# Attention of neighbouring heads in the two partition halves, logits in the output banks

## What is computed

```python
# fox branch, for one block of 128 queries
logits = einsum('bthd,bshd->bhts', qb, k) * HEAD_DIM ** -0.5 + fb - cum_k
p = softmax(where(key_pos <= t_pos, logits, NEG))
o = einsum('bhts,bshd->bthd', p, v)
# latent branch: the same with keys and values expanded from a latent of 128,
# a T5 bias, and all but the top 64 keys of each query masked by a score
```

## Time and profile before

| | |
|---|---|
| median of the runs | 1445.54 us |
| the profiled execution | 1447.23 us, its span 1445.1 us |
| PE (matmul) busy | 1403.2 us, 97% of the span |
| DVE, ACT, POOL busy | 939.4, 785.2, 134.6 us |
| DMA | 243 MB, mean 168 GB/s |

### The profile page before, as it was taken

One profiled execution on the slowest core, in us unless ns is written; L12 is line 12 of the kernel. 1 busy time (PEld: TensorE's weight loads), 2 busy tenths in 40 slices (PEclk: granted clock), 3 DMA queues, 4 the chain that ended last, 5 costly groups with the idle time before them and its releaser, 6 DMA issues.

```text
span 1445.1 us, 23849 instructions
## 1 busy us (share of the span) xinstructions
PE 1403.2 (97%) x8845; PEld 1249.3 (86%) x8845; DVE 939.4 (65%) x1451; ACT 785.2 (54%) x1376; POOL 134.6 (9%) x223
## 2 busy tenths in 40 slices
PE   5999989999999999999999999999999999999997
PEld 5888879988999888888888888899989999888886
DVE  4666665867566557666676666658666566666665
ACT  5455555755554556555565555565547445655543
POOL 2010000022320100000000000000224001000001
PEclk9999999999999999999999999999999999999999
DMA  8678664543435555666566567445344454465661
GB/s 219 190 202 210 187 181 146 176 146 129 152 129 176 174 143 155 198 180 198 175 177 201 175 188 214 141 154 168 120 154 136 146 184 145 138 204 176 199 180 71
DMA packets 286064, 243.38 MB, mean 168 GB/s; under 512 B 14280, under 2 KB 263544, under 8 KB 285984
## 3 DMA queue, kind: packets, MB, share of 16 engines
q1 hardware_dynamic: 283856, 236.77, 53.7%
q10 hardware_dynamic: 1600, 4.25, 0.8%
q0 software_dynamic: 528, 1.26, 0.6%
HBM read 241.18 MB, written 1.27 MB: 168 GB/s over the span
## 4 chain that ended last, share of the span: by engine, by line
issue 62%; PE 29%; DVE 3%; POOL 1%; ACT 1%; DMA 1%; POOLq 1%; DVEq 1%; ACTq 0%
PE work L1507 17%; PE work L1582 2%; PE work L1727 2%; PE work L1529 2%; PE work L1716 2%; PE work L1584 1%; PE acc L1544 1%; POOL diag L702 1%; PE work L1707 1%; DVE score L1308 1%; POOLq L701 1%; DMA gains_in<-in_mem_norm 1%; PE work L1651 0%; PE acc L1458 0%; DVE w_lo L504 0%
## 5 line engine op out<-in xcount | busy, mean ns | idle before, releaser
L504 DVE TENSOR_TENSOR w_lo<-raw,w_hi 128x1024 fp32r<-128x1024 f32 x444 | 537.7, 1231 | 104.2 <-ACT w_hi L496 102.3
L1582 PE MATMUL work<-act,w_hi 128*128 128x512 f32 x1408 | 499.4, 398 | 8.3 <-DVE w_lo L504 4.3
L496 ACT ACTIVATE w_hi<-raw 128x1024 fp32r<-128x1024 f32 x444 | 452.5, 1052 | 26.0 <-PE acc L1544 25.6
L1584 PE MATMUL work<-act,w_lo 128*128 128x256 f32 x1408 | 395.8, 281 | 0.0
L1582 PEld LDWEIGHTS work<-act,w_hi 128*128 128x128 f32 x1408 | 265.3, 188 | 72.9 <-issue 9.3
L1507 PE MATMUL work<-act,w_hi 128*128 128x256 f32 x1696 | 317.2, 286 | 4.7 <-DVE o_lo L1366 2.2
L1507 PEld LDWEIGHTS work<-act,w_hi 128*128 128x128 f32 x1696 | 267.5, 192 | 12.4 <-issue 6.3
L1584 PEld LDWEIGHTS work<-act,w_lo 128*128 128x128 f32 x1408 | 267.0, 190 | 1.6
L1507 PE MATMUL work<-act,w_lo 128*128 128x256 f32 x848 | 239.8, 283 | 0.0
L803 ACT ACTIVATE gu_s<-work 128x256 f32<-128x256 f32 x176 | 58.0, 382 | 209.6 <-PE work L1584 209.6
L1507 PEld LDWEIGHTS work<-act,w_lo 128*128 128x128 f32 x848 | 162.5, 192 | 0.1
(11 more groups left out here) (232 smaller groups left out, 1771.6 us busy)
## 6 DMA issues: line engine op xcount, KB each, us to landing
raw<-in_ffn_w_gu SPq DMA_DIRECT2D x176, 512.0 KB, 4.9
raw<-in_w_in SPq DMA_DIRECT2D x52, 1024.0 KB, 5.0
raw<-in_ffn_w_down SPq DMA_DIRECT2D x44, 1024.0 KB, 4.8
raw<-in_w_branch SPq DMA_DIRECT2D x12, 1024.0 KB, 4.9
raw<-in_w_mkv SPq DMA_DIRECT2D x8, 1024.0 KB, 5.1
raw<-in_w_out SPq DMA_DIRECT2D x8, 1024.0 KB, 4.8
raw<-in_w_mq SPq DMA_DIRECT2D x4, 1024.0 KB, 5.0
raw<-in_w_mo SPq DMA_DIRECT2D x4, 1024.0 KB, 4.9
```

Source lines behind the costliest of these rows:

```text
L496: eng.activation(halves(w_hi, slot, kind, part), halves(raw, slot, kind, part), ACT.Copy)\
L504: eng.tensor_tensor(halves(w_lo, slot, kind, part), halves(raw, slot, kind, part), halves(w_hi, slot, kind, part).bitcast(F32), ALU.subtra ...
L1582: pe.matmul(work[:, 2 * c + g, :], w_hi[:, slot, at_w:at_w + P], act[:, :, k, :], start=(k == 0), stop=False, skip_group_check=True)
L1584: mm = pe.matmul(work[:, 2 * c + g, 0:SEQ], w_lo[:, slot, at_w:at_w + P], act_hi[:, k, :], start=False, stop=(k == KT - 1), skip_group_che ...
```

## The change

The two heads of a stream slot become neighbours, 2·pr and 2·pr+1, one in each half of the partitions, in the same tile. The logits go to `acc`, one bank for each head, two banks for even slots and two for odd; the `qk` jobs leave the turn of the `work` banks, and PE waits for the extreme (`lg_ready`) of slot s-2 instead of a bank. The two `pv` products write the two halves of the partitions, the same columns, and their order is chunk by chunk with the heads inside. ACT and DVE take `pv` out as 128 partitions of 128 in place of 64 partitions of 256. The index slots keep their pairs.

```diff
+def idx_slot_of(k):
+    blk, pr = k // 4, k % 4
+    h = IDX_PAIRS[pr][0]
+    return blk, h, HD * (h % 2), h // 2
 def slot_of(k):
-    blk, pr = (k % 8) // 4, k % 4
-    h = HEAD_PAIRS[pr][0]
-    return blk, h, HD * (h % 2), h // 2
+    return (k % 8) // 4, k % 4
...
             if s < STREAM:
-                self.job(("qk", s))
+                self.acc_job(("qk", s))
...
+        def logits(s):
+            return acc[:, s % 2, :].rearrange("p (h n) -> p h n", h=2)[:, :, 0:P * (slot_of(s)[0] + 1)]
...
-                        a.activation(o_hi[k < 8][base:base + HD, m:m + 2, blk * P:blk * P + P],
-                                     ps(("pv", k))[base:base + HD, 0:2 * P].rearrange("p (h t) -> p h t", h=2),
-                                     ACT.Copy).then_inc(o_part, 1)
+                        a.activation(o_hi[k < 8][:, pr, blk * P:blk * P + P], ps(("pv", k))[:, 0:P], ACT.Copy)\
+                         .then_inc(o_part, 1)
...
-                            v.scalar_tensor_tensor(out=lgs, in0=ps2(("qk", s))[:, :, 0:s_len], scalar=-HD ** -0.5,
-                                                   in1=fox_bias[:, h:h + 3:2, 0:s_len], op0=ALU.mult, op1=ALU.add)\
-                             .then_inc(bank_of(("qk", s)), 1)
+                            v.scalar_tensor_tensor(out=lgs, in0=logits(s), scalar=-HD ** -0.5,
+                                                   in1=fox_bias[:, 2 * pr:2 * pr + 2, 0:s_len], op0=ALU.mult,
+                                                   op1=ALU.add)
...
-                        dst = (slice(base, base + HD), slice(m, m + 2), slice(blk * P, blk * P + P))
-                        v.tensor_tensor(o_lo[k < 8][dst], ps(("pv", k))[base:base + HD, 0:2 * P].rearrange("p (h t) -> p h t", h=2),
-                                        o_hi[k < 8][dst].bitcast(F32), ALU.subtract).then_inc(bank_of(("pv", k)), 1)
+                        dst = (slice(0, P), pr, slice(blk * P, blk * P + P))
+                        v.tensor_tensor(o_lo[k < 8][dst], ps(("pv", k))[:, 0:P], o_hi[k < 8][dst].bitcast(F32),
+                                        ALU.subtract).then_inc(bank_of(("pv", k)), 1)
...
-                        for j in range(2):
-                            for c in range(blk + 1):
-                                mm = pe.matmul(ps(("pv", k))[base:base + HD, j * P:j * P + P],
-                                               values[:, c, (h + 2 * j) * HD:(h + 2 * j + 1) * HD],
+                        for c in range(blk + 1):
+                            for j in range(2):
+                                mm = pe.matmul(ps(("pv", k))[HD * j:HD * j + HD, 0:P],
+                                               values[:, c, (2 * pr + j) * HD:(2 * pr + j + 1) * HD],
                                                pt[:, k % 2, j, c, :], start=(c == 0), stop=(c == blk))
...
-                        wait_jobs(pe, l, [f"qc{m // 2}", f"kc{m // 2}"] if s < 8 else [f"qb{m // 2}", ("kb", m // 2)],
-                                  ("qk", s))
+                        wait_jobs(pe, l, [f"qc{pr // 2}", f"kc{pr // 2}"] if s < 8 else [f"qb{pr // 2}", ("kb", pr // 2)])
+                        if s >= 2:
+                            pe.wait_ge(lg_ready, l * STREAM + s - 1)
                         for j in range(2):
-                            mm = pe.matmul(ps2(("qk", s))[:, j, 0:s_len], queries[base:base + HD, m + j, blk * P:blk * P + P],
-                                           keys[base:base + HD, m + j, 0:s_len], start=True, stop=True)
+                            mm = pe.matmul(logits(s)[:, j, :], queries[HD * j:HD * j + HD, pr, blk * P:blk * P + P],
+                                           keys[HD * j:HD * j + HD, pr, 0:s_len], start=True, stop=True)
```

More of the change, by code:

```diff
@@ L68 @@
 SSQ = sum(SUMS_OF)
-HEAD_PAIRS = ((0, 2), (1, 3), (4, 6), (5, 7))
+IDX_PAIRS = ((0, 2), (1, 3), (4, 6), (5, 7))
 STREAM = 16
@@ L707, in causal_bias @@
             def causal_bias(pr):
-                h = HEAD_PAIRS[pr][0]
-                heads = fox_bias[:, h:h + 3:2, P:SEQ]
+                heads = fox_bias[:, 2 * pr:2 * pr + 2, P:SEQ]
                 g.tensor_tensor(heads, heads, causal[:, P:SEQ].unsqueeze(1).to_broadcast([P, 2, P]), ALU.subtract)\
@@ L714, in bias_and_score @@
             def bias_and_score(l, s):
-                blk, h, base, m = slot_of(s)
+                blk, pr = slot_of(s)
                 s_len = P * (blk + 1)
@@ L722, in bias_and_score @@
                 g.wait_ge(lg_ready, l * STREAM + s - 1)
-                g.tensor_tensor(t5_score[:, s % 2, :, 0:s_len], t5[:, h:h + 3:2, SEQ - s_len:SEQ],
+                g.tensor_tensor(t5_score[:, s % 2, :, 0:s_len], t5[:, 2 * pr:2 * pr + 2, SEQ - s_len:SEQ],
                                 score[:, blk, 0:s_len].unsqueeze(1).to_broadcast([P, 2, s_len]), ALU.add)\
@@ L973, in _ @@
                 for i in range(IDX_SLOTS):
-                    blk, h, base, m = slot_of(i)
+                    blk, h, base, m = idx_slot_of(i)
                     s_len = P * (blk + 1)
@@ L998, in _ @@
                         k = s - 2
-                        blk, h, base, m = slot_of(k)
+                        blk, pr = slot_of(k)
                         wait_done(a, l, ("pv", k))
-                        a.activation(o_hi[k < 8][base:base + HD, m:m + 2, blk * P:blk * P + P],
-                                     ps(("pv", k))[base:base + HD, 0:2 * P].rearrange("p (h t) -> p h t", h=2),
-                                     ACT.Copy).then_inc(o_part, 1)
+                        a.activation(o_hi[k < 8][:, pr, blk * P:blk * P + P], ps(("pv", k))[:, 0:P], ACT.Copy)\
+                         .then_inc(o_part, 1)
                     if s >= 1:
@@ L1350, in _ @@
                             v.wait_ge(t5_score_ready, l * 8 + s - 7)
-                            v.scalar_tensor_tensor(out=lgs, in0=ps2(("qk", s))[:, :, 0:s_len], scalar=-HD ** -0.5,
-                                                   in1=t5_score[:, s % 2, :, 0:s_len], op0=ALU.mult, op1=ALU.subtract)\
-                             .then_inc(bank_of(("qk", s)), 1)
+                            v.scalar_tensor_tensor(out=lgs, in0=logits(s), scalar=-HD ** -0.5,
+                                                   in1=t5_score[:, s % 2, :, 0:s_len], op0=ALU.mult, op1=ALU.subtract)
                         v.drain()
```

4 lines of the change are left out of this document (2 added, 2 removed).

## The result

The changed kernel took 1421.36, 1425.74, 1426.10 and 1426.34 us, median 1425.92; the kernel before, in the same comparison, 1445.08 (median of four). The ratio is 0.9864, its interval 0.9849 to 0.9879: 1.4% faster, as forecast, by 19.2 us where 21.1 was said. The profiled execution took 1426.34 us with a span of 1424.2, against 1447.23 and 1445.1 before, so by the executions whose traces are compared the gain is 20.9 us.

The account below looks back on a forecast made before the run. PE, busy 97% of the span, was taken to bound the kernel. Savings of 9.7 + 9.3 + 2.4 less 0.3 gave 21.1 us, so 1445.5 - 21.1 = 1424.4 us, range 1422.5 to 1434.5.

Parts of the forecast that it names:

- The products of queries and keys: PE's qk in the streams: 0.64 falls to 0.43 us in block 0, 1.06 to 0.64 in block 1; saves 9.7 us.
- That slot 0 gains nothing: First slot of each stream: DVE reaches the logits late, so PE still waits; takes 2 x 0.2 us off the saving.
- The products with the values: PE's pv in the streams: column halves save between 0 and 9.3 us; the upper end was taken.
- The argument by the feed: For pv: two streams of 128 columns in 0.11 us are no faster than a filler's 256 four-byte columns in 0.12.
- The turn of the banks: Step 8 of each layer: filler ga3 no longer waits for DVE's o_lo to free its bank; 2.4 us in two layers.
- The other new neighbours: Other jobs' banks in the new turn: freed a step earlier or by ACT at step start, gc2 the closest; no wait priced.
- I expect 2.27 in all block 1 slots: POOL's product was to take 2.27 us in odd slots too, where it took 1.04, leaving 1.2 less slack there.
- The softmax term: Transposes waiting for POOL's product once PE comes earlier: a loss of 0 to 1.4 us, taken as 0.3.
- The sum: Whole kernel: 9.7 + 9.3 + 2.4 - 0.3 = 21.1 us saved.
- the forecast's own range: 1422.5 us, with nothing lost in steps 1 and 16 nor to POOL, to 1425.8 us; chance 0.64.

Follow-up runs that it names:

- run 1: Changed kernel with both value products written to the lower 64 partitions again, side by side, taken out by two instructions each: 1436.31 us, ratio 0.9924.
- run 3: Changed kernel with the value products issued head outside, chunk inside, as in the kernel before: 1427.98 us, ratio 0.9874.
- Run 2: Kernel before with only the logits in acc and qk out of the turn of banks, heads paired as before: 1442.36 us, ratio 0.9966.
- Run 4: Changed kernel with fillers ga2, gc2 and gb0 put in the bank of the same step's transposes, which ACT frees: 1421.86 us, ratio 0.9828.
- Run 6: Changed kernel with o_lo moved behind the second half of DVE's split: 1423.38 us, ratio 0.9834.
- run 5: The changed kernel unaltered, timed once more: 1426.93 us, ratio 0.9867.

## Why the prediction was right, and where it was not

**The products of queries and keys: right.** 0.43 and 0.64 were forecast from the index slots, 0.422 and 0.633 measured. That slot 0 gains nothing is right too: PE's wait for the chain there grew by the 0.2 us that the product lost.

**The products with the values: right, at the upper bound.** 0.37 and 0.59 were forecast and measured, and run 1 prices them at 8.7 to 10.4 us against 9.3. The argument by the feed (a filler takes in 256 columns of four bytes where the two heads take in two streams of 128) pointed the right way, though no row had shown column halves; taking the upper bound of 0 to 9.3 was a bet that came off. The Trainium skill's rule of strict order ("TensorE: Matmul & The Clock Gate", section "The mechanism") fails here for column halves as it did for row halves: run 3 issues four and four, and they run side by side.

**The turn of the banks: right in itself.** Run 2 took the wait for `o_lo` away and 1.3 us off a stream, where 1.2 was said (1.09 to 1.25 for the stall; from start to start it was worth 1.36).

**The other new neighbours: wrong.** This is the step that failed: "The other new neighbours are freed a step earlier or by ACT at the start of the step". `gc2`, called the closest, waits 0.4 us, and `ga2`, which was not named at all, 0.4 and in layer 1 0.5; 0.8 to 0.9 us a layer that the sum did not have. `gb0` waits 0.6, 0.4 more than before, as said. Run 4 takes all three away and finds 1.5 us a stream.

**DVE and POOL: wrong, and the cause of the step above.** "I expect 2.27 in all block 1 slots" put the loss on POOL, which has slack. It fell on DVE, whose split took 2.10 for 1.21 in the even slots, and DVE's merges are what the fillers wait for. Run 6, where POOL loses beside every split, leaves 0.3 of 1.5 us. The Trainium skill's rule on held instructions ("VectorE: DVE Perf Modes", section "Two Vector instructions with no wait between them") was right: `o_lo` now starts 0.08 us behind the reciprocal's start in all slots (331.08, 331.16), as it did in the even slots before. What I concluded from it was wrong. The shorter `o_lo` brings the split to 0.27 behind the reciprocal, 0.03 behind POOL's start (331.32, 331.35), where POOL mostly wins; I had looked only at `o_lo` against POOL, and not worked out when the split comes. The idea itself, that an earlier split wins, fails as well: at 0.40 DVE won in all 14 even slots of the kernel before that have an `o_lo`, at 0.27 it mostly loses. Why is open.

**The softmax term: 0.3 taken, nothing found.** POOL kept 1.04, and no transpose but the first waits.

**The sum.** In a layer the products save 8 x 0.216 + 8 x 0.425 + 8 x 0.212 + 8 x 0.431 = 10.3 us. PE's waits grew by 0.4 us in layer 0 and 0.5 in layer 1: 9.9 and 9.7, and 9.96 and 9.83 were measured (9.53 and 9.40 for the stream, and 0.43 for the last product). Read from start to start, a wait is worth more than its idle time on both sides: the stall of `ga3` gave back 1.36, and `gc2` took 0.67. Forecast were 10.55. That the traces differ by 20.9, so close to 21.1, is partly luck: 1.3 us of unforeseen loss against 1.2 of a load that came earlier. The median of the changed kernel, 1425.92, is 1.5 above the forecast and inside the stated range, 1422.5 to 1434.5, but just above the forecast's own range, which ended at 1425.8. By their terms the ends should read 1422.9 (10.1 + 10.1 + 2.4), 1425.5 and 1434.8, which changes nothing.

**Left open.** Whether each head's logits need a bank of their own was not tried: with both in one bank, the two row halves of the array would write it at once. (The column halves of `pv` do write one bank, each its own 64 partitions.) The toss between DVE and POOL is shown, not what decides it.

## What to carry to other kernels

Two heads of 64 in the two halves of the array, rows or columns, run side by side at no price in order or switches that these runs show, and the products then took 58 to 66% of their time; look at a place of the same kernel where such tiles already follow each other before doubting it. When one engine is brought forward by a tenth of a slot, list for every job who frees its bank and how late that engine is: the waits here came where PE was 0.5 us earlier or the freeing engine 0.8 later. And when a DVE instruction with two SBUF inputs starts near a GpSimd one, work out both start times, and price the loss on either of them.

## What the runs showed of the hardware

**Halves of the array.** Float32 passes in two column halves start 0.007 us apart and cost one chain, interleaved (0.587) or head by head (0.594); the order of issue is worth 0.007 us. No drain at a change of half is seen in any of the 64 products.

**DVE against POOL.** When both want two SBUF inputs, one waits: the split goes from 1.21 to 2.10 with a POOL product of 1.04, or the product from 1.04 to 2.27 with a split of 1.21. It is the loser's end that is fixed, not its length: the split ended 1.09 us behind POOL's product whether it had started 0.27 or 0.66 behind the reciprocal, and POOL's product 0.90 behind the split, at lengths of 2.27 (before) and 1.94 (run 6). The Trainium skill ("SBUF — State Buffer", section "Who interferes with whom") says that whichever issues first gets the shared ports for its whole instruction. The lengths agree with that; the recorded starts don't tell who is first. POOL's product started 0.03 us ahead of the split and won (331.32, 331.35); in slot 6 of the kernel before it started at 343.18, 0.16 ahead of the split at 343.34, and lost; and the same slot of the same kernel went 1.04 in one execution and 2.14 in the next (run 5).

**The clock.** Although PE is 97% busy, the granted clock fell to 1.2 GHz for stretches of 3.4 or 6.8 us (and for longer ones behind its last instruction). Each of them in the twelve traces began during an idle time of PE or shortly behind one (in run 1 PE was idle from 296.13 to 297.80, and the clock was at 1.2 GHz from 298.3 to 301.7, 0.57 granted over 298 to 302 us). The places are the same few in every trace; which of them are hit changes from one execution to the next, though PE sits idle there about as long each time.
